# A 64-row state update padded to 128 rows in a two-layer decoder step

## The reference

```python
k_end = kc * jnp.exp(b_last[:, None] - b)
...
S = jnp.exp(b_last)[..., None] * S + jnp.einsum('bshk,bshv->bhkv', k_end, vc)
```

## Time and profile before

| | |
|---|---|
| median of 3 runs | 1342.97 us (1339.02 to 1348.56) |
| the profiled execution's own time | 1344.02 us |
| its span | 1342.1 us |
| mean granted clock of TensorE | 0.967 |
| busy: PE, Pool, DVE, ACT | 95%, 53%, 49%, 42% |
| the DMA queues together | 192.11 MB, 143 GB/s in the mean |

### The profile page before, as it was taken

The page is one execution under the profiler, slowest core; times in us unless marked ns, Lnnn a source line. Parts: engine busy times, 40 slices in busy tenths (PEclk is TensorE's granted clock), DMA queues, the critical chain, the costliest instruction groups (busy, mean ns, idle before and its releaser), DMA issues.

```text
span 1342.1 us, 20963 instructions
## 1 busy us (share of the span) xinstructions
PE 1280.7 (95%) x8240; PEld 1219.1 (91%) x8240; DVE 651.4 (49%) x1203; ACT 569.3 (42%) x926; POOL 710.4 (53%) x298
## 2 busy tenths in 40 slices
PE   3899998999999999999988999989999999999995
PEld 2799888989999999999968988979899999999995
DVE  5534426457386543144263542476446854412425
ACT  5363323234434554255444622334335355534542
POOL 2552333345466666666655333335336666767672
PEclk9899998989999999999988999989899999999998
DMA  8434342233344444444654343333324444444451
GB/s 305 153 117 178 135 142 95 96 130 126 110 143 143 150 147 154 146 157 142 212 186 142 121 178 126 112 128 126 98 96 145 145 151 143 157 144 155 144 193 56
DMA packets 53379, 192.11 MB, mean 143 GB/s; under 512 B 6048, under 2 KB 7328, under 8 KB 52896
## 3 DMA queue, kind: packets, MB, share of 16 engines
q1 hardware_dynamic: 43632, 159.15, 34.9%
q10 hardware_dynamic: 9648, 31.60, 6.6%
HBM read 182.20 MB, written 8.53 MB: 142 GB/s over the span
## 4 chain that ended last, share of the span: by engine, by line
PE 88%; DVE 8%; ACT 2%; issue 1%; DMA 1%; POOL 0%; DVEq 0%; SPq 0%; ACTq 0%; POOLq 0%
PE bank L944 40%; PE bank L975 30%; PE bank L988 6%; PE bank L1169 2%; DVE arena L633 1%; PE bank L1059 1%; PE bank L1072 1%; DVE arena L608 1%; PE bank L1158 1%; DVE hl L645 1%; DVE arena L815 1%; PE bank L1188 1%; DVE arena L829 1%; PE bank L1192 1%; PE bank L1181 1%
## 5 line engine op out<-in xcount | busy, mean ns | idle before, releaser
L225 POOL TENSOR_TENSOR wlo<-raw,whi 128x1024 fp32r<-128x1024 f32 x294 | 710.2, 2416 | 612.1 <-PE bank L975 341.7
L255 ACT ACTIVATE whi<-raw 128x1024 fp32r<-128x1024 f32 x294 | 310.4, 1056 | 319.5 <-PE bank L944 171.7
L975 PE MATMUL bank<-oh,whi 128*128 128x320 f32 x848 | 287.4, 339 | 18.7 <-DVE arena L747 8.5
L975 PE MATMUL bank<-ol,whi 128*128 128x320 f32 x848 | 284.5, 336 | 0.0
L975 PE MATMUL bank<-oh,wlo 128*128 128x320 f32 x848 | 283.9, 335 | 0.0
L944 PE MATMUL bank<-hh,whi 128*128 128x320 f32 x832 | 257.8, 310 | 0.1
L944 PE MATMUL bank<-hl,whi 128*128 128x320 f32 x832 | 257.1, 309 | 0.0
L944 PE MATMUL bank<-hh,wlo 128*128 128x320 f32 x832 | 257.1, 309 | 0.0
L975 PEld LDWEIGHTS bank<-oh,whi 128*128 128x128 f32 x848 | 167.9, 198 | 27.1 <-DVE ol L637 9.3
L975 PEld LDWEIGHTS bank<-oh,wlo 128*128 128x128 f32 x848 | 167.8, 198 | 3.6 <-issue 1.6
L975 PEld LDWEIGHTS bank<-ol,whi 128*128 128x128 f32 x848 | 168.0, 198 | 3.2 <-issue 0.4
(11 more groups left out here) (188 smaller groups left out, 1756.6 us busy)
## 6 DMA issues: line engine op xcount, KB each, us to landing
raw<-w SPq DMA_DIRECT2D x296, 512.0 KB, 3.2
arena<-cache_k ACTq DMA_DIRECT2D x16, 512.0 KB, 5.3
arena<-cache_v ACTq DMA_DIRECT2D x16, 512.0 KB, 4.3
arena<-st_in ACTq DMA_DIRECT2D x8, 512.0 KB, 4.4
sst_out<-arena ACTq DMA_DIRECT2D x8, 512.0 KB, 2.7
arena<-mem_in ACTq DMA_DIRECT2D x2, 1024.0 KB, 6.5
con<-consts SPq DMA_DIRECT2D x1, 1288.0 KB, 13.0
x<-x_in SPq DMA_DIRECT2D x2, 640.0 KB, 8.8
```

The costliest lines, as they stand in the source:

```text
L225: pool.tensor_tensor(out=wlo[:, u % 2, :], in0=raw[:, u % 4, :], in1=whi[:, u % 4, :].bitcast(f32), op=ALU.subtract).then_inc(lo_ready, 1)
L255: nc.scalar.activation(whi[:, s, :], raw[:, s, :], ACT.Copy).then_inc(hi_ready, 1)
L975: r = MM(o, a, b[:, k, 0:n], start=k == 0 and i == 0, stop=k == KT_ - 1 and i == 2, skip_group_check=True)
```

## The change

L1169 multiplies all 128 partitions of `kTm` and `vt` instead of the upper 64. So that the rows of prompt tokens add nothing, the lower 64 rows of `kTm` are set to zero, once, in the prologue. PE's wait ahead of the pairs counts this memset too. Nothing else is changed; the part of the kernel named with it in the change's title, the up-projection, is the same before and after.

```diff
@@ -595,6 +595,7 @@
             V.memset(zp[:, 1:2], GEPS).then_inc(prol, 1)
             for e in range(2):
                 V.memset(qz[64 - 64 * e:128 - 64 * e, e, :], 0.0).then_inc(qz_zero, 1)
+            V.memset(kTm[0:64, :, :], 0.0).then_inc(qz_zero, 1)
 
             def add_square(j, n0, width=T):
 
@@ -1166,8 +1167,8 @@
                         return
                     j, e = i // 2, i % 2
                     h = 2 * (p % 2) + e
-                    r = MM(B[2 + j // 2][:, (j % 2 * 2 + e) * P:(j % 2 * 2 + e + 1) * P], kTm[64:128, e, j * P:(j + 1) * P],
-                           vt[64:128, p // 2, 2, h * P:(h + 1) * P], start=True, stop=True, skip_group_check=True)
+                    r = MM(B[2 + j // 2][:, (j % 2 * 2 + e) * P:(j % 2 * 2 + e + 1) * P], kTm[:, e, j * P:(j + 1) * P],
+                           vt[:, p // 2, 2, h * P:(h + 1) * P], start=True, stop=True, skip_group_check=True)
                     if i == DEC_BATCH - 1:
                         r.then_inc(us_done, 1)
 
@@ -1194,7 +1195,7 @@
                         if b == 7:
                             r.then_inc(o_done, 1)
 
-                pe.wait_ge(qz_zero, 2)
+                pe.wait_ge(qz_zero, 3)
                 for p in range(4):
                     u = U_SIL + 8 * p
                     pe.wait_ge(ktc_ready, lv * 16 + 4 * p + 4)
```

## The result

The changed kernel takes 1302.4 us as the median of four runs (1302.0 to 1303.0), and 1302.8 us as the median of five more beside later experiments (1301.8 to 1304.2). The kernel before took 1344.9 us as the median of four runs on the same chip (1339.0 to 1348.6). The ratio is 0.9688, with a 95% interval of 0.9651 to 0.9726: faster by about 3%. The forecast was 1302 us, with a range of 1294 to 1311 us.

What follows compares the result with a forecast made beforehand. TensorE's instruction stream plus its lowered clock was taken as the bound. Steps of 24.8 us and clock of 16.2 us gave 41.0 us saved, so 1343.0 - 41.0 = 1302 us, range 1294 to 1311 us.

Steps and rivals of the forecast that it cites:

- What bounds the kernel: Whole kernel: TensorE, busy 95% of the span, sets the time by its instruction stream, plus what the lower clock adds.
- The price of a small call: TensorE at L1169 and L1158: a small call costs 0.61 us with 64 rows, 0.22 us with 128.
- the first section of the prediction: At L1169: TensorE does not overlap work across a change between 128 and 64 rows, 3.1 us in a unit.
- The new unit taken from unit u: Eight units holding L1169 take 5.30 us each, like those holding L1158: 83.1 us become 42.4, saving 40.7 us.
- the head of the one unit u+3: One unit right behind an L1169 unit, begun at half clock: 8.72 us become 8.37, saving 0.35 us.
- The clock: In the units holding L1169 the clock no longer falls to half: 16.2 us of the 41.0 us saved.
- 0.86 against 0.06: Units holding L1169: chance of the full gain (1302 us) against the rival that the clock falls all the same (1318 us).
- The memset: Added 64 x 1024 zeroing on VectorE in the prologue: at most 1.2 us, hidden by idle time, taken as nothing.
- What becomes late next: Unit behind each L1169 unit: its waits for VectorE, sample state and weights stay covered; the 4.25 us stall stays.
- The silu of the first pair: VectorE ends it at 196.62 us, the new L1169 unit ends at 197.98 us: 1.4 us are left.
- a spread: Four low-clock stretches after stalls, 3.4 us more or less in each, move the time by up to 7 us.

Runs made afterwards that it cites:

- The dose of two, four and six calls: Changed kernel with two, four or six of each unit's eight sample updates back at 64 rows: 1310.9, 1317.7 and 1320.4 us.
- the batched kernel: Kernel before, still 64 rows, with all eight small calls of a unit in one row behind its first large product: 1306.7 us.
- the order alone: Changed kernel with VectorE's fifth silu ahead of the second pair's operands and its sixth ahead of the reciprocals: 1300.5 us.
- the order with work taken off the engine: Changed kernel with both VectorE silus moved earlier and the padded-query copies of pairs 1 to 3 made by ScalarE: 1290.7 us.

## Why the prediction was right

*What bounds the kernel.* It held. PE is busy for 42.5 us less, and the span is 41.2 us shorter. The row of clocks was read too finely, though: a 9 in it stands for 90% or more, and of the eight slices below that only four lie in the parts with head pairs. The windows of single units carried the argument, not this row.

*The price of a small call.* It was read as 0.61 against 0.22 us, from the starts and not from the durations. The dose of two, four and six calls gave 0.38 to 0.39 us for each, and the batched kernel shows that the price belongs to the change of rows, as the first section of the prediction has it. This was an inference from one pattern then; it is shown now, in both halves of the partitions, in two places, with 64 and with 16 rows. The rule of the Trainium skill that a change of tiling mode drains TensorE ("TensorEngine Tiling (Array Packing)", "Key Properties") agrees with all of it, at 0.38 us for there and back here. The traces show the gap and not what fills it. What the Trainium skill states of loads ("TensorE: Matmul & The Clock Gate", "LDWEIGHTS (loading the stationary operand)"), that one with few rows takes as long as one with all, agrees as well (medians of 186 and 190 ns), and taken alone it would have misled.

*The new unit taken from unit u.* 5.30 us was forecast and 5.30 us came, eight times; 42.4 us in the sum. One small term was mis-sized: the 0.35 us for the head of the one unit u+3. The 8.37 us that it was measured against hold 25 large products, since that window opens one product early (253.24 instead of 253.40 us). With 24 that unit takes 8.21 us, and the unit u+3 in question went from 8.72 to 8.22 us, a saving of 0.50 us. In the same way the eight units u+2 before come to 83.3 us instead of 83.1 us when each window holds 24 large products. The sum should have been 41.4 us instead of 41.0 us, which changes nothing in the forecast of 1302 us.

*The clock.* 16.2 us were put down to it, as what was left of the sum. The straight line of the doses leaves 14 to 20 us, depending on which runs of before are taken. By their mean clocks the eight units u+2 before hold some 36 us at half clock, and half of that, 18 us, is the most it can have cost. That the clock would stay up (0.86 against 0.06) was argued from unit u alone, and held.

*The memset.* At most 1.2 us of DVE, hidden; it took 0.91 us, from 1.95 us on, with 4.97 us of idle time behind it. On DVE it was hidden, as forecast.

*What becomes late next.* The silu of the first pair was to end 1.4 us ahead of the end of u+2. It ended 1.36 us ahead (197.73 against 199.09). The low stretch at the stall came out as 3.4 us in both layers of the profile after, where the second layer had 6.8 us. From the start of the first unit u on, the span got shorter by 42.3 us (1159.4 to 1117.1 us), 0.9 us more than the 41.4 us; the second layer's shorter low stretch gives 0.8 us (its first pair without unit u+2 took 40.3 us and takes 39.4 us). Ahead of that unit 1.1 us were lost, as ScalarE had to wait 0.85 us for the first activations. Whether the added memset has a part in this isn't settled. The two profiled kernels without it start that unit at 182.6 and 182.7 us and don't wait there; the twelve with it start it between 182.6 and 185.1 us, and in two of these ScalarE doesn't wait there either. These two parts, which the forecast had as a spread, happened to cancel: that it is right to within 1 us is partly luck, and the 3% are not.

## What to carry to other kernels

Look at the spacing of starts on TensorE, not at durations, where products with fewer rows stand alone among full ones: each change of the row count there and back cost 0.38 us here, more than the small call itself (0.22 us). Pad such operands with zeros to the full rows, or lay the calls with few rows in one row, which won all but 4 us of the same gain. If a wait for another engine is moved by reordering that engine's work, look at what stands in the queue next; here the order alone gave 2 us, and the order with work taken off the engine 12 us.

## What the runs showed of the hardware that was not expected

The clock did not fall in proportion to the gaps. Six isolated 64-row calls of eight, with a unit 44% longer than without gaps (7.62 us), kept it at 1.00 in every unit u+2, and eight of eight brought it down in every one, at a cost of about two thirds of that of the gaps themselves (16 against 25 us).

The kernels whose clock falls in the pairs also spread more from run to run: the kernel before lay between 1338 and 1349 us in all its runs, the changed one in nine runs between 1301.8 and 1304.2 us. The spread goes with the time at low clock: of the 38 runs of the kernel before beside the experiments, the nine above 1347 us had a mean granted clock of 0.964 or 0.965, and those below 1342 us one of 0.969 to 0.974. That the stretches in the units u+2 make this difference fits the profiles, where each is 3.4 or 6.8 us long for the same pattern of work; no run shows it directly.
